# Prompts' parts of the value compression moved among the last key unit's chunks, branch products split, first inverse moved

## The reference

```python
def _compress(k, pos_emb, w1, w2):           # keys and values, prompt and samples
    ch = k[:, :n_chunk * 16].reshape(B, n_chunk, 16, N_KV, HEAD_DIM)
    first = einsum('bcsgd,sdh->bcgh', ch + pos_emb[:16], w1[:16])
    second = einsum('bcsgd,sdh->bcgh', ch + pos_emb[16:], w1[16:])
    hid = silu(first[:, :-1] + second[:, 1:])
    return einsum('bngh,hd->bngd', hid, w2)
yb = gates[0] * o_cmp + gates[1] * o_selected + gates[2] * o_window
x = x + (sig(g_a) * (silu(za) * ya) @ w_out_a + sig(g_b) * (silu(zb) * yb) @ w_out_b) @ w_o
```

## Time and profile before

| | us |
|---|---|
| median of 3 runs | 2262.25 |
| lowest, highest | 2257.63, 2263.7 |
| the profiled execution | 2269.26 |
| its span, first to last instruction | 2267.5 |

### The profile page before, as it was taken

The page is one execution under the profiler, slowest core; times in us unless marked ns, Lnnn a source line. Parts: engine busy times, 40 slices in busy tenths (PEclk is TensorE's granted clock), DMA queues, the critical chain, the costliest instruction groups (busy, mean ns, idle before and its releaser), DMA issues.

```text
span 2267.5 us, 46106 instructions
## 1 busy us (share of the span) xinstructions
PE 2180.8 (96%) x17635; PEld 1958.0 (86%) x17635; DVE 1463.7 (65%) x2978; ACT 1015.4 (45%) x1936; POOL 216.9 (10%) x357
## 2 busy tenths in 40 slices
PE   8999999999999899899999999999999999998997
PEld 8999999999889555599999999999998984554997
DVE  5888565557686766654478776555667766666544
ACT  5333333536554666533243333334446455665232
POOL 0000000000000333400000000000000003334000
PEclk9999999999999999999999999999999999999999
DMA  6655476844311877843345645777152219779421
GB/s 227 188 165 158 117 207 155 203 125 153 112 57 38 141 120 131 197 148 113 102 138 158 190 123 140 205 186 212 37 190 94 75 25 144 113 120 223 152 94 40
DMA packets 405539, 312.69 MB, mean 138 GB/s; under 512 B 224281, under 2 KB 376281, under 8 KB 404040
## 3 DMA queue, kind: packets, MB, share of 16 engines
q1 hardware_dynamic: 399752, 268.70, 47.2%
q0 software_dynamic: 5568, 41.05, 5.1%
HBM read 282.80 MB, written 77.09 MB: 159 GB/s over the span
## 4 chain that ended last, share of the span: by engine, by line
PE 78%; DVE 9%; DMA 4%; SPq 3%; ACT 2%; issue 2%; DVEq 2%; POOL 1%; ACTq 0%; POOLq 0%
PE ps L1016 31%; PE ps L1004 12%; PE ps L1197 6%; PE ps L1276 5%; PE ps L1297 3%; PE ps L1441 3%; PE ps L1410 2%; PE ps L1465 2%; SPq L751 2%; PE ps L1222 2%; PE ps L1561 2%; PE ps L1716 1%; PE ps L1191 1%; DVE chL L2728 1%; DMA zbs<-zb_keep 1%
## 5 line engine op out<-in xcount | busy, mean ns | idle before, releaser
L454 DVE TENSOR_TENSOR wL<-w_raw,wH 128x2048 fp32r<-128x2048 f32 (+1 forms) x77 | 176.9, 2298 | 112.5 <-ACT wH L448 112.3
L1016 PE MATMUL ps<-hH,wH 128*128 128x272 f32 x1088 | 225.6, 289 | 2.2 <-DVE wL L454 2.1
L1016 PE MATMUL ps<-hH,wL 128*128 128x272 f32 x1088 | 226.2, 289 | 0.0
L1016 PE MATMUL ps<-hL,wH 128*128 128x272 f32 x1088 | 224.9, 288 | 0.0
L473 ACT ACTIVATE wpH<-w_raw 128x512 fp32r<-128x512 f32 x168 | 102.0, 623 | 171.8 <-DMA w_raw<-in_w_in 101.9
L1016 PEld LDWEIGHTS ps<-hH,wH 128*128 128x128 f32 x1088 | 171.4, 189 | 3.3 <-DVE wL L454 3.3
L1016 PEld LDWEIGHTS ps<-hH,wL 128*128 128x128 f32 x1088 | 170.9, 189 | 0.0
L1016 PEld LDWEIGHTS ps<-hL,wH 128*128 128x128 f32 x1088 | 170.6, 188 | 0.0
L448 ACT ACTIVATE wH<-w_raw 128x2048 fp32r<-128x2048 f32 (+1 forms) x77 | 147.5, 1916 | 21.2 <-DMA w_raw<-in_w_in 16.4
L948 POOL TENSOR_SCALAR pr<-pr,inv,zg 128x512 f32<-128x512 f32 (+2 forms) x192 | 119.8, 633 | 358.6 <-DVE inv L3025 358.6
L1276 PE MATMUL ps<-chH,w1H 128*128 128x256 f32 x512 | 148.1, 289 | 0.0
(11 more groups left out here) (431 smaller groups left out, 5926.0 us busy)
## 6 DMA issues: line engine op xcount, KB each, us to landing
w_raw<-in_w_in SPq DMA_DIRECT2D x59, 1024.0 KB
rows_keep<-in_cache_kv SPq DMA_DIRECT2D x256, 128.0 KB, 3.4
craw<-rows_keep SPq DMA_DIRECT2D x32, 1024.0 KB, 7.4
w_raw<-in_w_in SPq DMA_DIRECT2D x64, 256.0 KB
k_sel<-in_cache_kv SPq DMA_DIRECT2D x128, 128.0 KB, 4.8
v_sel<-in_cache_kv SPq DMA_DIRECT2D x128, 128.0 KB, 8.7
out_new_win_sample<-in_state_win POOLq DMA_DIRECT2D x16, 1016.0 KB, 5.3
w_raw<-in_w_out_a SPq DMA_DIRECT2D x8, 1024.0 KB
```

The lines of the kernel that those rows point to most:

```text
L454: dve.tensor_tensor(block_part(wL, b), block_part(w_raw, b), block_part(wH, b).bitcast(F32), ALU.subtract).then_inc(w_lo, 1)
L1016: last = nc.tensor.matmul(ps[:, bank + hf, 0:HALF], st, x[:, k, hf * HALF:(hf + 1) * HALF], start=k == 0 and w is wH and x is xH, stop=k = ...
```

## The change

Three edits, which alter only the order of work on an engine:
- `prompts_high(5, j)` and `prompts_low(5, j)`, with the wait for kv_out before them, go from behind unit 4's last step to places among its steps: part 0 before `unit_start(4)`, part 1 behind it, part 2 behind the first value weight and before step (4, 3), part 3 behind step (4, 3).
- GpSimd's seven branch products in a row after unit 58's scaling become four there, one after unit 60's and two after unit 63's.
- `inverses(0)` stands before `hidden_sums(9)` in VectorE's order, instead of behind it.

```diff
@@ GpSimd, in the loop over the 64 units
                     if i == 58:
                         pool.wait_ge(zb_back, 16 * l + 16)
                         pool.wait_ge(pa_o, 8 * l + 7)
-                        for c in range(KT - 1):
+                        for c in range(4):
                             branch(c)
+                    elif i == 60:
+                        branch(4)
+                branch(5)
+                branch(6)
@@ ScalarE
-                unit_start(4)
-                w1_high(1, 0)
-                chunk_parts(4, 3)
                 act.wait_ge(kv_out, 160 * l + 160)
                 prompts_high(5, 0)
+                unit_start(4)
+                prompts_high(5, 1)
+                w1_high(1, 0)
+                prompts_high(5, 2)
+                chunk_parts(4, 3)
+                prompts_high(5, 3)
                 odd_chunks(6, 0)
-                prompts_high(5, 1)
                 w1_high(1, 1)
                 w1_high(1, 2)
                 chunks_high(6, 0)
-                prompts_high(5, 2)
                 w1_high(1, 3)
-                prompts_high(5, 3)
                 second_part(4)
@@ VectorE
-                unit_start(4)
-                w1_low(1, 0)
-                chunk_parts(4, 3)
                 dve.wait_ge(kv_out, 160 * l + 160)
                 prompts_low(5, 0)
+                unit_start(4)
+                prompts_low(5, 1)
+                w1_low(1, 0)
+                prompts_low(5, 2)
+                chunk_parts(4, 3)
+                prompts_low(5, 3)
                 chunk_sum(6, 0)
-                prompts_low(5, 1)
                 w1_low(1, 1)
                 w1_low(1, 2)
-                prompts_low(5, 2)
                 w1_low(1, 3)
-                prompts_low(5, 3)
                 hidden_sums(4)
@@ VectorE, at the start of the attention
                 maxima(0)
                 maxima(1)
+                inverses(0)
                 hidden_sums(9)
-                inverses(0)
                 maxima(2)
                 hidden(9)
```

## The result

The changed kernel takes 2274.04 us (median of 15 runs, 2268.86 to 2282.9), the kernel before 2263.82 (15 runs on the same chip). The ratio is 1.0039, 95% interval 1.0028 to 1.005: slower by about 8.8 us (6.3 to 11.3). The forecast was 2260.4 with "no change" as the likeliest, and a range of 2250 to 2270; the time lies above it. It is the side of the third rival (2268.5), which had 0.17.

The account below looks back on a forecast made before the run. TensorE, busy 96% of the span, bounds the kernel; only its idle and low-clock time can be gained. Prompts' parts + 8.2, branch products - 7.1, inverse - 3.0 sum to - 1.9: median 2260.4, range 2250 to 2270.

Parts of the forecast that it names:

- the third rival: Unit 4: chunks wait for prompts' parts, clock falls at all three idles; +6.3, 2268.5, deciding from 5.1 per layer; chance 0.17.
- no change: Whole kernel: time stays within 0.3%, 6.8 us; chance 0.55.
- (+1.4) ... (+1.4): Units 4 to 6: low-clock loss behind the idle of 4.8 and again behind that of 3.3, 1.4 us each.
- the idle of 2.5: Before the transposes at 611.11, layer 0: TensorE idle grows from 0.70 to 2.5 us; no clock loss counted there.
- 1.3 + 1.4 + 1.4 = 4.1 per layer: Prompts' parts: VectorE's queue 1.3 us later plus two clock losses of 1.4; 8.2 us lost in two layers.
- The second rival: Prompts' parts find room on both engines, gaining 10.4, 2241.8; against it, VectorE's gaps of 1.15 are under a part's 1.75; chance 0.08.
- 3.4 and 3.7 us: Branch products near unit 59: gains in layer 0 and layer 1 from four GpSimd products instead of seven; 7.1 in sum.
- the last two are done at 963.2; ScalarE's reads of those chunks come after 967: GpSimd's last two branch products, layer 0: finished at 963.2, before ScalarE reads their chunks after 967.
- would go with the products: VectorE beside GpSimd's seven products: the 0.64 us wait on the shared port would go when products are moved.
- a gain nearer 8.4: Branch products: gain nearer the bound of 8.4 than 7.1 if the shared-port wait goes too.
- instead of 749.07: 1.5 gained: After unit 0's turn: the next unit's turn waits until 747.5 instead of 749.07; 1.5 us gained per layer, 3.0 in sum.
- 0 (the slack goes to a later wait): First inverse sooner: lower bound of the 3.0 us gain, zero if the slack goes to a later wait; upper bound 6.

Follow-up runs that it names:

- the filled kernel: Changed kernel plus useless identity transposes in two TensorE idle times per layer, before chunk (6,0)'s transposes and unit 6's joint product; ratio 0.9991 to the kernel before.
- 0.9956 against 0.9976: Kernel before with prompts' parts placed one at a time and unit 4's compressed copy moved earlier on VectorE: 0.9956 with the branch and inverse edits, 0.9976 without.
- The kernel with the spread parts and the copy alone: Kernel before with part 0 before chunk (4,0) is summed, others behind chunk (4,3), and unit 4's compressed copy ahead of unit 5's hidden sums on VectorE; 0.9976.

## Why the prediction was wrong

**Change 1, the number of clock falls.** The mechanism was right: who waits, for whom, and within 0.6 us how long. What failed is the step "(+1.4) ... (+1.4). I take these two and not the idle of 2.5: 1.3 + 1.4 + 1.4 = 4.1 per layer". I gave each of two idle times one fall, four falls in all. A stretch of ten microseconds with one fall has a mean clock of 0.83, that is 3.4 us at 1.2 GHz; one of 0.66 has two. The changed kernel has seven in the two stretches: in layer 0 one behind the 4.88 and two at the 2.74, in layer 1 one behind the 2.46 that I left out (its eight transposes took 1.97), two behind the 4.56 and one at the 2.73.

The sum can be read off, counted from the mark at unit 4's start. The joint product came 2.97 us later than before in layer 0 and 5.36 in layer 1 (forecast 1.3 + 1.4 = 2.7), and from there to the keys' transposes another 2.64 and 1.41 were lost (forecast 1.4). The terms themselves were sized well. In the filled kernel the joint product came 2.93 and 2.23 later, with the one fall behind the 2.46 in each layer; against layer 0 of the changed kernel, which has no fall there, that fall delays the transposes for (6,0) by 1.37 and 0.84. An estimate from these rows: 1.6 and 1.4 per layer for the order (forecast 1.3), and the remaining 9.4 of the 12.4 over seven falls, 1.35 each (forecast 1.4). The falls of the profile before, two and one, cost its joint product nothing, as I had said: it stands 45.2 us behind the mark with two and 45.3 with one. So the price was right and the count was not.

Over the five kernels that have part 0 where the change has it, the idle of 2.46 brought a fall in eight layers of ten; leaving it out was no fair guess. The third rival came nearest: it had 8.2 per layer for falls at all three idle times and a point of decision of 5.1, which both layers passed. By its own terms (2.8 lost in 6.7 us) it would have been 1.3 + 3 x 2.8 = 9.7.

The second rival's "each gap is shorter than a part" was also wrong for one gap, the 2.41 us shown above, and a faster kernel came of it.

**Change 2: the wait went, and half of the gain with it.** I had 3.4 and 3.7 us; the single edit measured 3.4 in all, and 0.9956 against 0.9976 says 4.5. In the changed kernel unit 59 no longer waits for GpSimd in layer 0, whose four products end at 956.4:

```profile
951.45 4.95 POOL L940 TENSOR_TENSOR zbs<-zbs,yT 128x512 f32<-128x512 f32 x4 [4.65 <-DMA zbs<-zb_keep]
```

(In the single edit's profile zb came back later and 1.95 us of that wait stayed in layer 0.) But TensorE now waits twice for VectorE's copies:

```profile
962.47 0.64 PE L1445 MATMUL ps<-con,pr 128*128 128x128 f32 x4 [1.51 <-DVE prT L3035]
...
967.80 0.41 PE L1445 MATMUL ps<-con,prT 128*128 128x128 f32 x2 [1.10 <-DVE prT L3035]
```

The steps that failed are "the last two are done at 963.2; ScalarE's reads of those chunks come after 967", which asked only who reads the products and not what runs beside them, and that the wait on the port "would go with the products". It moved along with them. VectorE's own product of zb with the attention's output, before and after:

```profile
964.75 0.42 DVE L3219 TENSOR_TENSOR zbs<-zbs,yT 128x256 f32<-128x256 f32 x1
```

```profile
966.00 1.33 DVE L3223 TENSOR_TENSOR zbs<-zbs,yT 128x256 f32<-128x256 f32 x1
```

It takes 1.33 in all 20 layers of the ten kernels with the split products, where GpSimd's last two run beside it, and 0.42 in the eight of the other four; the weight's low part behind it takes 1.44 instead of 0.68. These 1.7 us lie in VectorE's queue around the last two copies that TensorE's turns wait for. Measured from VectorE's last copy of the samples' probabilities (spT) ahead of unit 58, the last turn comes 3.1 us sooner in the mean with the split products (20.9 instead of 24.0), near the forecast, but the first product of w_out_b only 2.0 (24.2 instead of 26.2): 4.0 in two layers, the size that was measured. More clock falls are not the cause: the profiles with the split products have 23 falls in these 20 places, the others 14 in 8. As far as they go, these rows agree with the rule that I cited, on the port that VectorE and GpSimd share (the Trainium skill, SBUF — State Buffer, SBUF: two separate sides); what was wrong is what I made of it, a gain nearer 8.4. No run kept the last two products clear of VectorE's work, so how much of the missing 2.6 to 3.7 us it would give back is not shown.

**Change 3: it gains nothing in the order.** With this edit alone the sample gates (zg) start 1.5 us sooner than in the profile before, as forecast, and the first turn that reads prT again at the old time. Both halves are the clock's. The step that failed is "instead of 749.07: 1.5 gained": what held unit 1's turn until 749.07 was a fall, in which the products ahead of it took 1.95 where they take 1.07 elsewhere:

```profile
746.49 1.95 PE L1323 MATMUL ps<-hidT,w 128*64 128x252 f32 x8
```

The kernel with the spread parts and the copy alone lacks this edit, idles the same 2.23 before unit 0's turn, and happened to have no fall there:

```profile
742.87 1.07 PE L1323 MATMUL ps<-hidT,w 128*64 128x252 f32 x8
...
746.89 1.09 PE L1477 MATMUL ps<-zg,con 32*128 32x48 f32 x8 [0.80 <-DVEq L2828]
```

Counted from the keys' transposes, its gates start at 91.36 us, those of the kernel with the edit alone at 91.36, those of before at 92.85. So the exact agreement with the forecast was luck. What the edit does is to cut the idle of 2.23 into 0.18, 1.40 and 0.62, and the fall that followed the whole one in five layers of eight comes some 7 us later, in 15 layers of 20, while TensorE is busy. From the kernel with this edit alone:

```profile
750.00:760.00 10.00, 10.00 (x118) 0.83 1.13 203
```

In layer 1 the changed kernel seemed to gain 3.0 us here. But the kernels without this edit (the prompts' alone, the branches' alone) reach the same mark 3.0 and 4.6 us sooner than the profiled execution of before as well. That one had two falls more than usual:

```profile
1860.00:1870.00 10.00, 6.97 (x40) 0.83 0.83 127
1870.00:1880.00 10.00, 10.00 (x112) 0.66 1.13 190
```

So the bound "0 (the slack goes to a later wait)" was the answer: of the 2.0 us that unit 0's turn comes sooner, 1.40 are waited again for unit 9's hidden values and 0.62 for ScalarE's copy.

**The base.** The profiled execution of before stood 5.4 us above the median of 15 runs, that of the changed kernel 1.1 below its own. The two profiles therefore differ by 3.6 us where the medians differ by 10.2. I scaled the forecast by subtraction, which was right for the sum (the base itself was 1.6 us low, 2262.25 from three runs against 2263.82), but had read single falls of that one execution (such as "only in layer 1") as properties of the kernel. The three edits alone measured +14.0, -3.4 and -0.9 where I had +8.2, -7.1 and -3.0: the misses are 5.8, 3.7 and 2.1 us, all on one side.

## What to carry to other kernels

Where TensorE is busy nearly all the time, an idle time costs its own length and then, if it is long, a clock fall (here, behind idle times over 2.1 us, in 108 of 123); price the second as well, and let the range take in one fall, two or none. Before moving work into an in-order queue, look for the place where that engine idles, between the very two items: the same part of 1.8 us cost nothing in a gap of 2.41 us, with ScalarE's half of it made a chunk sooner, and its whole length one instruction later, where the gap was 1.15; two parts beside a weight cost 4.0. Work moved off one engine's wait may slow what another engine does at the new place: look at the lengths there as well as at the readers. Where an idle time can't be removed, useless products in a free bank can be cheaper than the silence, and they are a good experiment to tell the clock's share from the order's. And a forecast that reads a gain off one profile should ask whether the time it removes was the order's or one fall's.

## What the runs showed of the hardware

Over the 14 profiles of this case, idle times of TensorE between 20 and 2200 us of the span, and whether the mean granted clock was under 0.95 in the 6 us behind:

| idle before | times | followed by a lower clock |
|---|---|---|
| 0.9 to 1.2 us | 45 | 0 |
| 1.2 to 1.6 | 75 | 20 |
| 1.6 to 2.1 | 31 | 10 |
| 2.1 to 2.6 | 85 | 70 |
| over 2.6 | 38 | 38 |

Some of the middle rows' falls belong to an idle time just ahead of them: counting only those that began with the idle time or behind it, the last four rows have 9, 10, 57 and 38. The same 2.46 or 2.58 us bring a fall in one execution or layer and none in the other, and single executions of the kernel before spread over 13 us (2257.63 to 2270.95). Part of that spread goes with the clock: over its 29 executions in the first set of experiments time and mean granted clock have a correlation of -0.75, with 1.2 us for each 0.001 of the clock. I had expected a fall after every idle of 2.2 and more, and one fall for each; an idle of 2.74 was followed by two (0.66 in 650 to 660).
